# All four down blocks of a gated FFN by seven corner products, spread over the next unit's gate and up phases, with corner sums by accumulating DMAs

## The reference

```python
def conv_gated_ffn(x, w_up, conv_w, conv_b, w_down):   # x (1, 256, 2048)
    gu = x @ w_up                                      # w_up (2048, 2*5632)
    gate, up = gu[..., :D_FF], gu[..., D_FF:]          # D_FF = 5632
    gate = causal_depthwise_conv(gate, conv_w, conv_b) # 3 taps along the tokens, plus a bias
    return (jax.nn.silu(gate) * up) @ w_down           # w_down (5632, 2048)

h = h + conv_gated_ffn(rms_norm(h, norm_ffn_g[i]), w_up[i], conv_w[i], conv_b[i], w_down[i])
```

## Time and profile before

| | |
|---|---|
| median of 3 runs | 2156.36 us (2156.32 to 2156.4) |
| the profiled execution | 2156.12 us |
| its span, first to last instruction | 2154.3 us |
| TensorE, VectorE, ScalarE busy | 2141.7, 1707.6, 1125.1 us |
| GpSimd busy | 50.4 us |
| DMA | 406.75 MB, mean 189 GB/s |

### The profile page before, as it was taken

One profiled execution on the slowest core, in us unless ns is written; L12 is line 12 of the kernel. 1 busy time (PEld: TensorE's weight loads), 2 busy tenths in 40 slices (PEclk: granted clock), 3 DMA queues, 4 the chain that ended last, 5 costly groups with the idle time before them and its releaser, 6 DMA issues.

```text
span 2154.3 us, 32719 instructions
## 1 busy us (share of the span) xinstructions
PE 2141.7 (99%) x11526; PEld 1859.3 (86%) x11526; DVE 1707.6 (79%) x2192; ACT 1125.1 (52%) x1422; POOL 50.4 (2%) x114
## 2 busy tenths in 40 slices
PE   9999999999999999999999999999999999999998
PEld 8898888888888888888898988888888888888886
DVE  5797569888889888897557875788888889888964
ACT  6556445554555544555554664445544545544554
POOL 2000000000000000000000000000000000000011
PEclk9999999999999999999999999999999999999999
DMA  8645555546555546555556455555556555556562
GB/s 269 213 139 174 178 200 188 182 158 233 205 204 178 182 166 234 197 192 195 173 183 182 138 176 176 201 203 176 186 177 234 195 197 176 183 185 234 176 216 97
DMA packets 233323, 406.75 MB, mean 189 GB/s; under 512 B 14828, under 2 KB 50268, under 8 KB 233096
## 3 DMA queue, kind: packets, MB, share of 16 engines
q1 hardware_dynamic: 231976, 402.72, 55.0%
q0 software_dynamic: 512, 1.76, 0.2%
q10 hardware_dynamic: 736, 1.07, 0.1%
HBM read 403.42 MB, written 2.10 MB: 188 GB/s over the span
## 4 chain that ended last, share of the span: by engine, by line
PE 97%; ACT 1%; DVE 1%; issue 1%; POOL 0%; POOLq 0%; DVEq 0%; ACTq 0%
PE acc L2082 16%; PE tps L2082 16%; PE acc L1901 12%; PE acc L1903 12%; PE acc L1902 12%; PE tps L2092 9%; PE acc L2092 9%; PE tps L1902 3%; PE tps L1903 3%; PE tps L1901 3%; PE acc L1988 1%; PE tps L1958 1%; ACT sq_h L773 0%; DVE h L1536 0%; DVE xb_lo L1193 0%
## 5 line engine op out<-in xcount | busy, mean ns | idle before, releaser
L996 ACT ACTIVATE w_hi<-raw 128x1024 fp32r<-128x1024 f32 x540 | 559.2, 1058 | 536.3 <-PE acc L2092 116.6
L1566 DVE TENSOR_TENSOR w_lo<-raw,w_hi 128x1024 fp32r<-128x1024 f32 x540 | 650.2, 1225 | 161.5 <-ACT w_hi L996 149.8
L1181 DVE TENSOR_TENSOR w_lo<-raw,w_hi 128x1024 fp32r<-128x1024 f32 (+1 forms) x288 | 342.0, 1211 | 143.2 <-ACT w_hi L722 137.6
L722 ACT ACTIVATE w_hi<-raw 128x1024 fp32r<-128x1024 f32 (+2 forms) x287 | 290.2, 1044 | 179.5 <-PE acc L1903 126.3
L2082 PE MATMUL acc<-xa,w_hi 128*128 128x512 f32 x1536 | 366.0, 391 | 0.0
L2082 PE MATMUL tps<-xa,w_hi 128*128 128x512 f32 x1536 | 361.2, 390 | 0.0
L2082 PEld LDWEIGHTS tps<-xa,w_hi 128*128 128x128 f32 x1536 | 285.3, 188 | 57.2
L2082 PEld LDWEIGHTS acc<-xa,w_hi 128*128 128x128 f32 x1536 | 283.7, 188 | 56.2 <-DVE h L1521 0.4
L1902 PE MATMUL acc<-w_hi,xb_lo 128*128 128x512 f32 x640 | 249.0, 389 | 0.0
L1901 PE MATMUL acc<-w_hi,xb_hi 128*128 128x512 f32 x560 | 220.5, 394 | 0.4 <-ACT pw L1072 0.4
L1903 PE MATMUL acc<-w_lo,xb_hi 128*128 128x512 f32 x560 | 218.1, 389 | 0.0
(11 more groups left out here) (262 smaller groups left out, 2651.1 us busy)
## 6 DMA issues: line engine op xcount, KB each, us to landing
raw<-in_w_up SPq DMA_DIRECT2D x176, 1024.0 KB, 5.0
raw<-in_w_down SPq DMA_DIRECT2D x88, 1024.0 KB, 5.0
raw<-in_w_out SPq DMA_DIRECT2D x32, 1024.0 KB, 5.0
raw<-in_w_ple_gate SPq DMA_DIRECT2D x32, 1024.0 KB, 5.1
raw<-in_w_in SPq DMA_DIRECT2D x21, 1024.0 KB, 5.4
raw<-in_w_ukv SPq DMA_DIRECT2D x8, 1024.0 KB, 5.5
raw<-in_w_in SPq DMA_DIRECT2D x8, 864.0 KB, 4.8
raw<-in_w_uq SPq DMA_DIRECT2D x6, 1024.0 KB, 5.7
```

Of the source, the lines that this page charges most:

```text
L722: copy(w_hi[:, half_of(m), 0:n], raw[:, c % RAW_SLOTS, at:at + n], ACT.Copy).then_inc(hi_done, 1)
L996: copy(w_hi[:, half_of(m), :], raw[:, c % RAW_SLOTS, half * HALF:(half + 1) * HALF], ACT.Copy).then_inc(hi_done, 1)
L1181: dve.tensor_tensor(w_lo[:, half_of(m), 0:n], raw[:, c % RAW_SLOTS, at:at + n], w_hi[:, half_of(m), 0:n].bitcast(F32), ALU.subtract).then_ ...
L1566: dve.tensor_tensor(w_lo[:, half_of(m), :], raw[:, slot, half * HALF:(half + 1) * HALF], w_hi[:, half_of(m), :].bitcast(F32), ALU.subtract ...
```

## The change

Per unit 1 to 10 and layer:

- All four down blocks go by seven products per pair: 14 corner products, no plain blocks. A unit has 30 halves. They are laid between the gate and up halves of the same unit's loop body, in two phases of 15: gate/up halves at 0, 1, 2, 3, 5, 8, 11, 14 of a phase (`X_AT`), corner products at 4, 6, 7, 9, 10, 12, 13 (`FORM_AT`). They work on the down product of the unit before.
- Chunk order in a phase: three of `w_up`, two of `w_down`, the fourth of `w_up`. A slot is free at its chunk's last split, `last_lo`: steps 1, 3, 8, 13, 12, 14 of a phase for chunks 0 to 5 (the first corner chunk, number 3, is held to step 13).
- ScalarE copies each product from PSUM to SBUF (`stage`, seven buffers of 128 x 512; `take`). Three of seven are added to `h` by VectorE from there (`from_stage`). Four are added to the corner sums by DMAs of GpSimd's queue with `accum_op=add` (256 KB each, 8 per unit).
- The last tap's multiplication with bias (`tap_2`) moves from VectorE to ScalarE. VectorE makes 8 weight differences instead of 4. The lo part of the last gated unit moves from GpSimd to VectorE.
- The last unit (`apart`) has its up phase unmixed: 8 up halves, then 7 products. Its body also folds the first pair's sums; the second pair's are folded behind it. The two blocks that were plain also get kept sums added in the tail.

```diff
-    UNIT_HALVES = 2 * UNIT_CHUNKS + CORNERS - 4
+    UNIT_HALVES = 2 * UNIT_CHUNKS + 2 * (CORNERS - 4)
+    PHASE = UNIT_HALVES // 2
...
+        X_AT = (0, 1, 2, 3, 5, 8, 11, 14)
+        FORM_AT = (4, 6, 7, 9, 10, 12, 13)
+        FORM_IN = {B11: (0, 0), B21: (0, 1), B22: (1, 1), T1: (0, 0), T3: (1, 0), T2: (1, 1), T4: (0, 1)}
+        Q_MIXED, X_MIXED = (3, 4), (0, 1, 2, 5)
...
+                def load_at(l, v, n, apart, pieces):
+                        freed = max(last_lo(n + 2 * RAW_SLOTS, False) + 1 - UNIT_HALVES, 2 * (n + 1) - 2 * RAW_SLOTS)
                     else:
-                        freed = 2 * (n - RAW_SLOTS) + 2
+                        freed = last_lo(n - RAW_SLOTS, apart) + 1
...
+                def products_added(v, second):
+                    for k, dst in ((B11, p1), (T1, p5), (T3, p7), (T2, p6)):
+                        pool.wait_ge(staged, taken(l, v, second, k + 1))
+                        pool.sem_inc(stage_seen, 1)
+                        pool.dma_start(dst, stage[:, k, :], accum_op=ALU.add).then_inc(added, 16)
+                    pool.wait_ge(added, 16 * 4 * phases(l, v, second))
+                    pool.sem_inc(stage_free, 1)
...
 ScalarE
+                    def take(second, k, bank, scale=None):
+                        if k == B11:
+                            act.wait_ge(stage_free, phases(l, v, second))
+                        copy(stage[:, k, :], bank, ACT.Copy).then_inc(staged, 1)
                     go(0, 2)
+                    up_low(u - 1, lambda: halves_used(act, l, M_UNIT - 1, v))
+                    go(2, 3)
                     copy(gt[0][:, :, :], conv[:, :, :], ACT.Copy).then_inc(g_hi, 1)
+                    go(3, 5)
                     copy(s_hi[:, :, :, :]...)
+                    go(5, 7); take(0, B11); go(7, 9); take(0, B21); go(9, 10); take(0, B22)
+                    go(10, 12); take(0, T1); go(12, 13); take(0, T3)
+                    go(13, 15); take(0, T2); take(0, T4)
+                    go(15, 17); gate_low(...)
+                    go(17, 19); tap_2(u); go(19, 21); silu(u)
+                    go(21, 22); take(1, B11); go(22, 24); take(1, B21); go(24, 25); take(1, B22)
+                    go(25, 27); take(1, T1); go(27, 28); take(1, T3)
+                    go(28, 30); take(1, T2); take(1, T4)
...
 VectorE
                     go(0, 2)
+                    up_sum(u - 1); gated(u - 1)
+                    go(2, 3); s_sums(v, 0); s_sums(v, 1)
                     lo(gt[1][:, :, :], conv[:, :, :], gt[0][:, :, :]).then_inc(g_lo, 1)
+                    s_sums(v, 2); s_sums(v, 3)
+                    go(3, 4); t_sum(v, 0, apart, 1); go(4, 5); t_sum(v, 0, apart, 2)
                     dve.tensor_tensor(s_lo ...).then_inc(s_split_lo, 1)
+                    go(5, 6); t_sum(v, 0, apart, 3); go(6, 7); t_sum(v, 0, apart, 4)
+                    go(7, 10); from_stage(0, B21); go(10, 12); from_stage(0, B22)
+                    go(12, 17); gate_sum(u, 0); gate_sum(u, 1); gate_normed(); from_stage(0, T4)
+                    go(17, 19); t_sum(v, 1, apart, 1); tap_1(u)
+                    go(19, 20); t_sum(v, 1, apart, 2); tap_0(u)
+                    go(20, 21); t_sum(v, 1, apart, 3); go(21, 22); t_sum(v, 1, apart, 4)
+                    go(22, 25); from_stage(1, B21); go(25, 27); from_stage(1, B22)
+                    go(27, 30); from_stage(1, T4)
...
 TensorE
+                    def gate_acc(f, first):
+                        if first:
+                            pe.wait_ge(staged, taken(l, v, 0, 0))
+                    def up_acc(f, first):
+                        if first:
+                            pe.wait_ge(staged, taken(l, v, 0, (5, 6, 7, 7)[f]))
+                    for i in range(8):
+                        x_half(X_AT[i], i, gate_acc, v)
+                        if i == 3:
+                            pe.wait_ge(g_lo, UNITS * l + u)
+                            product(0, B11, tps[:, 0, :])
+                        elif i == 4:
+                            product(0, B21, tps[:, 1, :])
+                            pe.wait_ge(s_split_lo, (UNITS - 1) * l + u)
+                            product(0, B22, tps[:, 2, :])
...
 tail
+                    if j < 2: add_block(l, bd + j, j, ((p1, p7), (p6, p5))[j])
```

More of the change, by code:

```diff
@@ new lines, in last_lo, with form_of, made, taken @@
+        def last_lo(c, apart):
+            return max(n for n in range(UNIT_HALVES) if raw_half(n, apart)[0] == c)
+        def form_of(n, apart):
+            form_at = FORM_APART if apart and n >= PHASE else FORM_AT
+            return form_at.index(n % PHASE) if n < UNIT_HALVES and n % PHASE in form_at else None
+        def made(l, v, second, k):
+            return 8 * (UNITS - 1) * l + 8 * v + (4 * second + k)
+        def taken(l, v, second, k):
+            return 2 * CORNERS * (UNITS - 1) * l + 2 * CORNERS * v + (CORNERS * second + k)
@@ L1674, in first_unit, with corners_summed @@
                     steps(l, m0 + 15, m0 + 16)
-                    up_sum(0)
-                    gated(0)
-                def unit(w, i):
-                    u = TURN_UNITS * w + (i + 1)
-                    m0 = M_UNIT + i * UNIT_HALVES
+                def corners_summed(second, k):
+                    p1, p7, p6, p5 = sums[second]
+                    dst, src = ((p6, p1), (p7, p6), (p6, p5), (p5, p7))[k]
+                    if k == 0:
+                        dve.wait_ge(stage_free, phases(l, UNITS - 2, second) + 1)
+                    else:
+                        dve.wait_ge(corner_folded, 8 * l + 4 * second + k)
+                    dve.tensor_tensor(dst, dst, src, ALU.add).then_inc(corner_folded, 1)
@@ L1696, in h_block, with from_stage @@
                     def h_block(t, j):
                         return h[:, t, j * BLK:(j + 1) * BLK]
+                    def from_stage(second, k):
+                        t, j = {B21: (0, 2 * second), B22: (0, 2 * second + 1), T4: (1, 2 * second)}[k]
+                        dve.wait_ge(staged, taken(l, v, second, k + 1))
+                        by_token(h_block(t, j), stage[:, k, :], t).then_inc(h_taken, 1)
                     go(0, 2)
+                    up_sum(u - 1)
+                    gated(u - 1)
@@ new lines, in product @@
+                    def product(second, k, bank):
+                        n = PHASE * second + (FORM_APART if apart and second else FORM_AT)[k]
+                        corner_product(M_UNIT + n, v, left[k], bank)
+                    def gate_acc(f, first):
+                        if first:
+                            pe.wait_ge(staged, taken(l, v, 0, 0))
+                        if first and f % 2 == 0:
+                            free_acc(l, b0 + f // 2, v)
+                        return acc[f // 2][:, f % 2, :]
@@ new lines, in unit @@
+                    for i in range(8):
+                        x_half(PHASE + X_APART[i], i, up_acc, v)
+                    block_split(l, b0, v)
+                    block_split(l, b0 + 1, v)
+                    product(1, B11, acc[0][:, 0, :])
+                    product(1, B21, acc[0][:, 1, :])
+                    product(1, B22, acc[1][:, 0, :])
+                    product(1, T1, acc[1][:, 1, :])
+                    pe.wait_ge(t_done, JOBS * l + (JB["p"] + T_BANKS))
+                    product(1, T3, tps[:, 0, :])
@@ L2409, in _ @@
+                    product(1, T2, tps[:, 1, :])
+                    product(1, T4, tps[:, 2, :])
                 jobs_split(l, JB["ffn_norm"] + 5)
                 first_unit()
-                with pe.Fori(0, LOOPS) as w:
-                    for i in range(TURN_UNITS):
-                        unit(w, i)
+                with pe.Fori(1, UNITS - 1) as u:
+                    unit(u, u - 1, False)
+                unit(UNITS - 1, UNITS - 2, True)
                 m, b = M_DOWN, BL["ple"] - N_BLK
```

541 lines of the change are left out of this document (325 added, 216 removed).

## The result

The changed kernel takes 2417.3 us (2415.0 to 2417.4) against 2156.3 us: ratio 1.121, 95% interval 1.119 to 1.123. It is slower, as forecast, but by 261 us where I had said 113, and 92 us above the upper end of the range. The profiled execution has a span of 2413.2 us.

The account below looks back on a forecast made before the run. Bound: a circle of late-released slots, load bunches and VectorE/ScalarE work, 71.1 us per unit with accumulating DMAs. Per layer 2.4 + 50.0 + 3 + 1 = 56.4; two layers +113 on 2156.1 gave 2269, stated as 2268, range 2150 to 2325.

Parts of the forecast that it names:

- The circle without collisions: VectorE/ScalarE loop from split 13 through split 28 to the next split 13, with both load bunches: 68.5 us per unit.
- the sum of the lower bound: Whole kernel if accumulating DMAs find holes between loads and cost nothing: 32 us per layer, 2221 in all.
- The dense rival: TensorE stays without gaps in the units, VectorE's 59.4 us fitting in 63.5: 2129 to 2135 us, chance 0.12.
- two per phase at 0.64 us: In each bunch of loads, two accumulating DMAs lengthen the third landing by their data time: 1.3 us per phase.
- b + 7.8: Time counted from b, the end of split 28; the next unit's corner chunk was forecast to land at b + 10.3.
- Its own 1.3 for T1 and T3: Middle estimate per phase for two accumulating DMAs whose data meets the three loads, 2 x 0.64 us.
- the upper bound: Accumulating DMAs in the bunches also read their destination, twice the data: 2.6 us per phase, 2316 in all.
- rival of slow DMAs: Accumulating DMAs over 4 us each fill the phase, ScalarE stands before B11: 2330 us and far more, chance 0.08.
- a second sum of 2305: Total if HBM loads were bound at about 358 GB/s: about 1 us more per bunch, 2 per unit.
- 6.25 for each of units 2 to 9: Added unit time, from a circle of 71.1 us against the period of 64.86: +50.0 us per layer.
- TensorE's saving: Down matmuls per unit fall from 90 to 84: 1.36 us per unit, 27.2 us over 20 units.
- the signs: Units near 71 us, TensorE idle 5 to 8, VectorE waiting for w_hi, third loads landing after 7 to 9.

Follow-up runs that it names:

- the last run: Late-issued DMAs, reordered lists, tail additions on VectorE behind its second block, copies T2 and T4 moved around a unit's last two splits, against the kernel before: 2154.2 us, ratio 0.9992.
- the group around `silu`: Moves of tap_2, tap_0 and silu, in the run that filled remaining waits (2172.5 us) and left out of the last run (2154.2 us).

## Why the prediction was right in sign and wrong in size

**Right: the bound.** The circle without collisions was 68.5; the run without the DMAs gives 67.8, the holes 1.61 and 2.68 stand where 1.6 and 2.9 were forecast, and its total is 2216.5 against 2221, the sum of the lower bound. The parts of that sum are near as well (TensorE's first gate matmuls, per layer): unit 1 costs 0.0 where it had 0.5, units 2 to 9 23.7 where it had 28.8, unit 10 with the tail 5.3 where it had 3. The work between them, 29.4 us, is 39.0 - 9.0 = 30.0 in the trace. The corner chunk holds the list from the slot that is released late, and TensorE has nothing to do with the length of the circle. The dense rival fell for the reason given: a VectorE list that fits into the unit does not help when it can't be worked through.

**The step that failed: the accumulating DMAs.** It was "two per phase at 0.64 us", 2.6 per unit; the runs show 10.2. Three parts:
- *The number.* Three are in each bunch. The prediction let the data come 3 us behind a copy. By its own times T2 is copied at b + 7.8 (5.2 to the first landing, 0.1, two splits, the copy), so its data comes at b + 10.8, only 0.5 behind the third landing at b + 10.3. Its own 1.3 for T1 and T3 moves that landing to b + 11.6, and then T2 is inside; this step was left out. In the trace T2 is issued at b + 9.0 (607.07) and the landing is at b + 15.5. Worth 2 x 0.64 = 1.3 per unit.
- *The price.* 1.44 us each, not 0.64: 6 x 0.80 = 4.8 per unit. Even the upper bound, twice the data, was 1.3 each, and the range took it for two DMAs a phase, 5.2 per unit, where six at 1.44 are 8.6. The prediction's rival of slow DMAs had its threshold at 4 us each and at `stage_free`; neither happened. ScalarE has no wait before B11 in the units of the changed kernel.
- *The rest*, 10.2 - 8.6 = 1.6 per unit, is not settled. That TensorE stands longer and loses its clock can't be it alone, since the circle holds no TensorE work. As plain copies six times 0.65 is 3.9 of 4.1, with half the columns six times 0.82 is 4.9 of 4.4, so the sum by six DMAs holds within 0.5 in those two and not in the change itself. One more thing is on the profiles' pages: the packets of the loads take longer too. Their queue has 49.2% of 2413.2 = 1187 us in the change, against 51.8% of 2214.1 = 1147 without the DMAs and 51.5% of 2229.3 = 1148 with them behind the bunch. That is 40 us, 2.0 per unit. But the same reckoning gives 0.9 for the copies and 1.3 for the halves, more than is left over there, and the shares pass 1, so packet times overlap: how much of the rest it is stays open.

The Trainium skill's page DMA: Bandwidth & Descriptors says, in its "Rules for kernel authors", that an accumulating DMA reads its destination and writes it later. The price is in keeping with that, 1.44 against 0.65 us, 2.2 times a copy; no run here shows the reading by itself. The section "Where 436 GB/s comes from" of the same page of the Trainium skill, by which the prediction had a second sum of 2305, has no part in the miss: once the additions are gone the loads again move 410 GB/s, in the window from 614 to 616.

**Unit by unit**, from one first gate matmul of TensorE to the next. The prediction had 6.25 for each of units 2 to 9; measured is 103.6 / 8 = 12.9 (374.41 to 996.79 against 368.25 to 887.08). For unit 1 it had 2.4, and measured is 6.0 (303.52 to 374.41, 70.9, against 303.40 to 368.25, 64.85). The slack that it gave the circle at its start is there: without the DMAs unit 1 still takes 64.8. Unit 10 and the tail together had 4, and measured are 19.6 (996.79 to 1501.83 against 887.08 to 1372.55), without the DMAs 5.3. The wait of 7.8 for `stage_free` before `xb_hi` is in it; how the rest divides is not shown. That is 129.2 per layer where the prediction had 56.4.

**TensorE's saving** was 1.36 per unit by count and pitch. In the last run TensorE's busy time over the whole execution is 2127.5 against 2141.7: 14.2, or 0.71 for each of 20 units, and the period is 64.07 (371.42 to 883.95, eight units), not 63.5. Part of it is that a product's matmul takes up to 0.228 between other halves, as here in the kernel with the additions of the tail on VectorE, 12 of them from

```profile
447.52 0.40 PE L2027 MATMUL tps<-w_hi,gt_hi 128*128 128x512 f32 x1
...
450.26 1.12 PE L2526 MATMUL acc<-xa,w_lo 128*128 128x256 f32 x8
```

in 2.74 us, against 0.2267 in the run of 90; 84 x 0.0016 is at most 0.13 (the next pair, from 453.06 to 455.78, runs at 0.2267). The rest, 0.4 per unit, I have not placed. So the most that this change brought TensorE is about half of what was counted: about 14 us, 0.7%. The tails take most of it back: in the last run units 1 to 9 of the first layer gain 7.2 (303.20 to 879.65 against 303.40 to 887.08), and unit 10 with the tail loses 4.8.

**What the signs should have shown.** The prediction said that GpSimd's transfers near 5 us would show it right; they landed 7.6 and 8.3 after issue in the median (5.0 and 5.4 when moved behind the bunch), and the loads of `w_down` 13.1 instead of 7 to 9. It also named a granted clock under full speed as a mechanism that it left out; the clock's mean is 0.979. I have not measured what that costs by itself: the circle doesn't run through TensorE, so in the units it should cost little.

## What to carry to other kernels

When a circle of releases and loads bounds a kernel, its length is the list's work plus its holes, and what lengthens a hole is whatever the DMA engines do between the release and the landing. Price each transfer by bytes and kind (an addition at twice a copy and more), place each against your own landing times, and put those that nobody waits for behind the bunch: here the same DMAs cost 10 us per unit inside it and 0.1 behind it. An edit that frees an engine which is not late is worth only what remains after the new order's holes, so check first which work can stand where the list will wait; and move one thing at a time: of several moves in one run, the group around `silu` cost 18 us and hid the gain of the rest.

## What the hardware showed that I had not expected

- An accumulating DMA of 256 KB from SBUF to SBUF takes 1.44 us of all 16 engines, a plain one 0.65, an accumulating one of half the size 0.82. It lands 3.2 us after issue at the quickest (the shortest of 80) and up to 11.8 us after it beside loads, in the median 7.6 and 8.3.
- DMA engines that are fully busy (share 1.02 to 1.09) moved only 259 to 352 GB/s with additions among the loads, 410 without: at the same share the throughput differed.
- TensorE was busy for 1.3 us from 604 to 608. Its granted clock was 0.73 in the second half of that stretch, 0.50 from 608 to 610, 0.92 from 610 to 612 and full from then on.
